# Retention's values two steps behind its scores, the convolution's norm beside the attention, and five smaller moves, in a three-block transformer kernel

## The chip, the cores and the metric

The kernel runs on one core of a Trainium2 chip. The metric is device time in microseconds (us) of one execution, median of three. Engine names: PE is TensorE (products), ACT is ScalarE (functions and copies out of PSUM), DVE is VectorE, POOL is GpSimd, SP issues most DMAs. PSUM has eight banks of 128x512 f32; a product writes a bank, and ACT or DVE empties it.

## What is computed

Sequence 512, width 1024. Two "hybrid" layers, then one block of another kind. A hybrid layer, cut to what matters here:

```python
def hybrid_layer(x, ...):
    u = rms_norm(x, g_mix_pre) @ w_in                 # aq ak av | cu | rq rk rv rg
    mix = concat([chunk_attention(aq, ak, av),        # 6 heads of 64
                  conv_module(cu), retention(rq, rk, rv, rg)]) @ w_out
    x = x + rms_norm(mix, g_mix_post)
    f = square(relu(rms_norm(x, g_mlp_pre) @ w_up)) @ w_down      # 4096 wide
    return x + rms_norm(f, g_mlp_post)

def conv_module(u):                                   # 256 channels, 31 taps
    y = causal_conv(a * sigmoid(gate)) + conv_b
    return silu(layer_norm(y) * ln_g + ln_b)

def retention(q, k, v, g):                            # 6 heads of 64, decayed causal scores
    q, k = rotary(q), rotary(k) / 8
    y = ((q @ k.T) * decay) @ v                       # what the chunked form amounts to
    return silu(g) * layer_norm(y)                    # one norm for each head
```

The last block has differential attention with 8 heads of value width 128 (each head's output is divided by its root mean square), a state-space layer whose parameters come from `exp`, `sin` and `cos` of small 128x16 tables and of their powers, gates, and an MLP.

## The kernel before

Each engine runs a program written out by hand (`products` for PE, `functions` for ACT, `arithmetic` for DVE, `low_parts` for POOL, `loads` for SP); semaphores join them. The order in which each function issues is the order on its engine, and an engine that waits holds back all that stands behind it on the same engine.

Large products are done in three passes of a reduced-precision form: weights and activations are both split in a high and a low part. SP loads a unit of weights (128x2048) to `raw`, ACT copies it to `w_hi` (`hi`, L1232), POOL subtracts to `w_lo` (`lo`, L509; for the very first unit in four pieces, `lo_pieces`, L501), and then PE may use it. There are two slots, so each chain load, copy, subtract of a unit runs beside the products of the unit before. For activations ACT writes `act_hi` and DVE `act_lo` (`split`, L1735; `low`, L1849).

**Start.** `first_norm` on ACT and the loop at the end of `arithmetic` on DVE take x in eight blocks k; `first_group` on PE (L762) does its first group k by k, twelve products for each k. At k = 7 it puts in the column means (L716) before output block 0 and the spread of the reciprocal root (`spread_rows`, L724) before output block 2. DVE's `turn_angles` (nine operations, L1920 to L1928) stands between block 1 and block 2. PE waits for `cmat`, a table of constant matrices, before its first product; its DMA is on ACT's queue behind block 1, and those of all eight x blocks are at ACT's start.

**Attention** of a hybrid layer is cut into steps i (head, query tile); `attention(i)` on each engine is put between pieces of the products for rq, rk, rv and rg (`attention_slots`), 26 slots and then the last steps together. Bank 3 is used by none of them while rq and rk are made.

**Retention** runs alone, with no large products beside it, until the first pieces of `w_out` (`OUT_STEPS`). Step i on PE: scores of step i into bank 4 or 5 (L771, `one`), values of step i - 1 (L798). Between them DVE multiplies the scores by `decay` out of PSUM into `pt` (L1807). The layer norms of the convolution (item 0) and of the three pairs of heads (items 1 to 3) are laid into the steps by `norm_steps`: mean on PE (L852), subtraction of the mean on DVE (L1860) and squares on ACT (L1389), variance on PE (L858), root on ACT and DVE, scaling, split. At step 2 DVE also splits the attention's three output blocks (L1849).

**MLP** of a hybrid layer: `up(g)` makes 512 hidden channels, `down(g)` adds their product with `w_down` to `f` in SBUF (L2023). In `up(0)` DVE clears `f` by a memset (L2013), and then runs `powers` (35 operations on 128x16, from L1939), the tables of the last block. It does so in both layers.

**Norms between parts** (`post_norm`): means, `busy(3)`, spread, `busy(12)`; `busy(n)` is n products of the identity with itself (L738) which nobody reads.

**Last block's attention**: for each step the scores, the turned probabilities (L1057, bank 6), the values (L1066), after a head's last step the mean of its squares (`one(6, m.avg128, ...)`, L771 with `att,cmat`, bank 6 too), and then `gate_piece(i)`, twelve large products.

```python
SEMAPHORE RULE, one(b, ...):  fill(b)            # wait until bank b was emptied
                              pe.matmul(...)     # then signal full<b>
retention, PE:   one(4 + i % 2, scores(i));  emptied(4 + (i - 1) % 2);  values(i - 1);  layer_norm(i)
```

## Time and profile before

| | us |
|---|---|
| median of 3 runs | 2418.72 |
| lowest, highest | 2415.46, 2423.01 |
| profiled execution, own time | 2415.07 |
| its span in the trace | 2413.2 |
| granted TensorE clock, mean | 0.965 of full |

Times below are in us from the span's start. A row of the timeline has start, duration, engine, line, operation, tiles and in brackets the idle time before it with what ended it. "x2" are two records; an f32 product shows as two. A product's duration is longer than its distance to the next, since products overlap; distances are what counts. 1.00 is PE's full clock (2.4 GHz), 0.50 its other level (1.2 GHz).

### The profile page before, as it was taken

To read this page: it belongs to the slowest core of one execution; us is meant where nothing else is said; L and a number is where in the kernel's file an instruction comes from. 1 tells how busy PE (TensorE), PEld (TensorE's weight loads), DVE (VectorE), ACT (ScalarE), POOL (GpSimd) and SP (SyncE) were. 2 spreads that over 40 slices of the span, in tenths; PEclk is the share of its full clock that TensorE was granted. 3 is DMA by queue.
4 is the path that set the end of the run, shared out by engine and by line. 5 is a ranking of instruction groups with operands and counts; after the bars stand their busy time and mean duration, and the time that the engine had idled before them with its cause. 6 is when DMAs were issued, how large, how long until landed. Compare 5 with 4: busy or idle time off the path is not lost.

```text
span 2413.2 us, 28705 instructions
## 1 busy us (share of the span) xinstructions
PE 2260.2 (94%) x10200; PEld 1729.8 (72%) x10200; DVE 1101.7 (46%) x1798; ACT 888.3 (37%) x1243; POOL 886.3 (37%) x274
## 2 busy tenths in 40 slices
PE   6999999999999998999999988977989789999999
PEld 4865487888878673778888866654766578788887
DVE  4844435221247444351222367674156652455445
ACT  4333343322343433532322332243255544333332
POOL 4522053343455221534444562321322135343443
PEclk9999899999999999999999998888999999999999
DMA  3412022323224220222232331011211113223232
GB/s 134 161 62 70 1 87 76 100 88 104 87 79 149 91 66 18 70 88 88 87 104 88 104 142 35 23 66 39 76 64 36 52 55 103 86 89 103 88 100 74
DMA packets 110587, 195.04 MB, mean 81 GB/s; under 512 B 4752, under 2 KB 41872, under 8 KB 110224
## 3 DMA queue, kind: packets, MB, share of 16 engines
q1 hardware_dynamic: 109184, 191.23, 24.2%
q10 hardware_dynamic: 1296, 2.43, 0.3%
q8 instruction: 63, 1.03, 0.2%
q14 instruction: 44, 0.36, 0.1%
HBM read 189.44 MB, written 8.12 MB: 82 GB/s over the span
## 4 chain that ended last, share of the span: by engine, by line
PE 69%; issue 21%; POOL 4%; DVE 4%; ACT 1%; DMA 1%; SPq 0%; POOLq 0%; DVEq 0%; ACTq 0%
PE bank L662 54%; POOL w_lo L509 4%; PE bank L771 4%; PE bank L762 3%; PE bank L798 1%; PE bank L835 1%; PE bank L959 1%; PE bank L826 1%; PE bank L858 1%; PE bank L716 1%; PE bank L738 1%; DVE b_pow L2076 0%; PE bank L990 0%; PE bank L852 0%; DMA lam<-in_lam 0%
## 5 line engine op out<-in xcount | busy, mean ns | idle before, releaser
L509 POOL TENSOR_TENSOR w_lo<-raw,w_hi 128x2048 fp32r<-128x2048 f32 (+1 forms) x167 | 740.4, 4434 | 1414.9 <-ACT w_hi L1232 1414.9
L662 PE MATMUL bank<-act_hi,w_hi 128*128 128x512 f32 x1488 | 605.9, 407 | 11.8 <-DVE act_lo L1849 4.4
L662 PE MATMUL bank<-act_lo,w_hi 128*128 128x512 f32 x1488 | 586.0, 394 | 0.0
L662 PE MATMUL bank<-act_hi,w_lo 128*128 128x512 f32 x1488 | 585.7, 394 | 0.0
L1232 ACT ACTIVATE w_hi<-raw 128x2048 fp32r<-128x2048 f32 (+1 forms) x170 | 314.1, 1848 | 641.5 <-PE bank L662 609.0
L662 PEld LDWEIGHTS bank<-act_hi,w_hi 128*128 128x128 f32 x1488 | 284.1, 191 | 93.8 <-issue 27.7
L662 PEld LDWEIGHTS bank<-act_lo,w_hi 128*128 128x128 f32 x1488 | 283.7, 191 | 63.6 <-issue 6.9
L662 PEld LDWEIGHTS bank<-act_hi,w_lo 128*128 128x128 f32 x1488 | 283.1, 190 | 61.1
L662 PE MATMUL bank<-h_hi,w_hi 128*128 128x512 f32 x736 | 298.7, 406 | 26.3 <-DVE h_lo L1849 17.7
L662 PE MATMUL bank<-h_lo,w_hi 128*128 128x512 f32 x736 | 294.6, 400 | 0.0
L662 PE MATMUL bank<-h_hi,w_lo 128*128 128x512 f32 x736 | 294.3, 400 | 0.0
L2023 DVE TENSOR_TENSOR f<-f,bank 128x512 f32<-128x512 f32 x128 | 87.4, 687 | 238.6 <-PE bank L662 238.6
L662 PEld LDWEIGHTS bank<-h_hi,w_hi 128*128 128x128 f32 x736 | 140.9, 191 | 66.3 <-DVE h_lo L1849 19.1
L662 PEld LDWEIGHTS bank<-h_lo,w_hi 128*128 128x128 f32 x736 | 141.1, 192 | 35.4 <-issue 1.5
L662 PEld LDWEIGHTS bank<-h_hi,w_lo 128*128 128x128 f32 x736 | 140.6, 191 | 35.0
L2008 DVE SCALAR_TENSOR_TENSOR hid<-bank,rrow 128x512 f32<-128x512 f32 x64 | 43.1, 690 | 233.8 <-PE bank L662 228.2
L762 PE MATMUL bank<-act_hi,w_hi 128*128 128x512 f32 x192 | 78.4, 408 | 27.1 <-POOL w_lo L501 16.8
L2300 DVE TENSOR_TENSOR bank<-bank,rrow 128x512 f32<-128x512 f32 x44 | 30.7, 699 | 142.7 <-PE bank L662 140.2
L525 POOL TENSOR_TENSOR sums<-sums,squares 128x512 f32<-128x512 f32 x50 | 64.9, 1298 | 46.4 <-ACT squares L1250 44.9
L1824 DVE CUSTOM_DVE_ANT_0 pr<-bank,btab 128x128 f32<-128x128 f32 (+3 forms) x48 | 23.6, 491 | 116.7 <-PE bank L771 116.0
L1784 DVE SCALAR_TENSOR_TENSOR bank<-ypad,lcol,bank 128x512 f32<-128x512 f32 x116 | 76.6, 750 | 0.0
L762 PE MATMUL bank<-act_hi,w_lo 128*128 128x512 f32 x192 | 76.5, 398 | 0.0
(321 smaller groups left out, 2835.8 us busy)
## 6 DMA issues: line engine op xcount, KB each, us to landing
raw<-in_w_up SPq DMA_DIRECT2D x32, 1024.0 KB, 5.1
raw<-in_w_down SPq DMA_DIRECT2D x32, 1024.0 KB, 5.1
raw<-in_w_in SPq DMA_DIRECT2D x26, 1024.0 KB, 5.2
raw<-in_w_up SPq DMA_DIRECT2D x44, 512.0 KB, 4.6
raw<-in_w_in SPq DMA_DIRECT2D x28, 768.0 KB, 4.5
raw<-in_w_out SPq DMA_DIRECT2D x12, 1024.0 KB, 5.1
raw<-in_w_down SPq DMA_DIRECT2D x22, 512.0 KB, 4.2
raw<-in_w_attn_proj SPq DMA_DIRECT2D x4, 1024.0 KB, 5.0
```

Source lines behind the costliest of these rows:

```text
L509: pool.tensor_tensor(m.w_lo[slot][:, 0:n], m.raw[slot][:, 0:n], m.w_hi[slot][:, 0:n].bitcast(F32), ALU.subtract).then_inc(s["split_ready"], 1)
L525: ins = pool.tensor_tensor(m.sums[:], m.sums[:], m.squares[n % 4][:], ALU.add)
L662: mm = pe.matmul(o, ll if i == 2 else lh, rl if i == 1 else rh, start=first and n == 0, stop=last and n == len(steps) - 1)
L716: mm = pe.matmul(bank[b][:, t:t + 1], x[:, t * P:(t + 1) * P], m.per_d, start=(part == 0), stop=(part == 1))
L738: pe.matmul(bank[1][:, 0:P], m.ident, m.ident, start=True, stop=True)
L762: mm = pe.matmul(bank[b][:], (wl if i == 2 else wh)[:, k % KU, cols], (m.act_lo if i == 1 else m.act_hi)[:, k, :], start=(k == 0 and i == ...
L771: pe.matmul(bank[b][:] if o is None else o, lhsT, rhs, start=True, stop=True).then_inc(s[f"full{b}"], 1)
L1232: act.activation(m.w_hi[slot][:, 0:n], m.raw[slot][:, 0:n], ACT.Copy).then_inc(s["w_hi"], 1)
L1784: ins = dve.scalar_tensor_tensor(to, y, w, sums, ALU.mult, ALU.add)
L2008: dve.scalar_tensor_tensor(m.hid[:, b, :], bank[b][:], 0.0, m.rrow[:], ALU.max, ALU.mult).then_inc(s[f"free{b}"], 1)
L2023: dve.tensor_tensor(sums, sums, bank[4 + b][:], ALU.add).then_inc(s[f"free{4 + b}"], 1)
L2300: dve.tensor_tensor(bank[b][:], bank[b][:], m.rrow[:], ALU.mult).then_inc(s["up_scaled"], 1)
```

## The change

- **Retention**: values stand two steps behind scores (`LAG = 2`), with scores in three banks in turn (4, 5, 1) and three buffers for the decayed scores (`pr`). The norms of the heads move by one step, the splits of items 1 and 2 by three more. The splits of the attention's output go to steps 5, 6 and 7, those of the convolution to 12 and 13.
- **Convolution's norm**: leaves retention's steps. Its mean, variance and root stand in attention steps 2, 4 and 6 with bank 3 (`conv_norm`); ACT's part with `Silu` (`conv_gate`) stands ahead of retention, in front of ACT's copy of the next weights.
- **Start**: x blocks 2 to 7 are loaded behind the directions and the first weight copy instead of at once, `tmul` on ACT's queue, `cmat` behind block 2. `turn_angles` stands before block 1, `powers` behind block 7, ahead of the reciprocal root. PE first does 14 products of `scol` which nobody reads, and waits for `cmat` only in `spread_rows`.
- **MLP**: `f` is cleared by two ACT copies with scale 0 behind `up(0)`'s last high part; DVE waits for them before its last low part. `powers` is gone from both layers.
- **Norms**: `busy(1)` in place of `busy(3)` between means and spread.
- **Last block**: the head's mean stands behind `gate_piece(i)` instead of before it.

```diff
 def retention():                                        # PE
-    one(4 + i % 2, m.rkT[...], m.rqT[...], bank[4 + i % 2][...])
-    if 1 <= i <= 6 * NT:
-        h, j = divmod(i - 1, NT)
+    one(SCORES[i % 3], m.rkT[...], m.rqT[...], bank[SCORES[i % 3]][...])
+    if LAG <= i < 6 * NT + LAG:
+        h, j = divmod(i - LAG, NT)
...
-        mm = pe.matmul(..., m.pt[:, (i - 1) % 2, 0:T - j * P], ...)
+        mm = pe.matmul(..., m.pr[:, (i - LAG) % 3, 0:T - j * P], ...)
...
+def conv_norm(i):                                       # PE; in attention steps
+    for stage in CONV_NORM.get(i, ()):
+        if stage in (MEAN, VARIANCE):
+            fill(CONV_BANK)
...
-NORM_BEGINS, NORM_STAGES = (1, 10, 18, 26), (0, 1, 3, 4, 7, 8)
+NORM_BEGINS, NORM_STAGES = (11, 19, 27), (0, 1, 3, 4, 7, 8)
+CONV_NORM = {2: (MEAN, CENTER), 4: (VARIANCE, ROOT), 6: (SCALE,)}
+Q_SPLIT, CONV_SPLIT = (5, 6, 7), (12, 13)
-BUSY = (3, 12)
+BUSY = (1, 12, 14)
...
+        if i < n_steps:                                 # PE, last block
+            gate_piece(i)
         if i >= 4 and (i - 4) % NT == NT - 1:
             pe.wait_ge(s["o_squared"], c.up("o_squared"))
             one(6, m.avg128, m.att[9][:])
-        if i < n_steps:
-            gate_piece(i)
...
+        conv_gate()                                     # ACT, ahead of retention
         hi()
...
+            if isinstance(g, int) and g == 0:           # ACT, up(0)
+                for half in range(2):
+                    act.activation(m.f[...4 blocks], m.eps.to_broadcast([P, 4 * T]), ACT.Copy, scale=0.0).then_inc(s["f_clear"], 1)
...
-            if isinstance(g, int) and g == 0:           # DVE, up(0)
-                link(dve.memset(m.f[:], 0.0))
-                powers()
...
     for k in range(KD):                                 # DVE, start
-        if k == 2:
+        if k == 1:
             turn_angles()
         split(k, new(k), gain("g0", m.scol, SC), False)
+    powers()
     root_row()
```

How it stands on the engines, at three places. First DVE's program at the start, before: `act_lo` is a split, `turn_102` to `turn_104` are work tiles of `turn_angles`.

```order
L1735 SCALAR_TENSOR_TENSOR act_lo<-bank,scol,act_hi 128x512 [waits act_hi,param_dve]
L1735 SCALAR_TENSOR_TENSOR act_lo<-bank,scol,act_hi 128x512 [waits act_hi]
L1920 TENSOR_TENSOR turn_102<-par,tmul 128x384
L1921 TENSOR_SCALAR turn_104<-turn_102 128x384 [waits param_dve]
L1922 SCALAR_TENSOR_TENSOR turn_102<-turn_104,turn_102 128x384 [waits param_dve]
```

The end of the same stretch after the change, still on DVE; L1984 is the last of `turn_angles`, L1995 the first of `powers`.

```order
L1984 SCALAR_TENSOR_TENSOR turn_table_68<-turn_104,turn_103 128x384 [waits param_dve]
L1777 SCALAR_TENSOR_TENSOR act_lo<-bank,scol,act_hi 128x512 [waits act_hi,param_dve]
L1777 SCALAR_TENSOR_TENSOR act_lo<-bank,scol,act_hi 128x512 [waits act_hi] x6
L1995 TENSOR_TENSOR par<-par 128x16 [waits param_act]
L1996 TENSOR_TENSOR par<-par 128x16 [waits dve_step]
```

So seven splits stand behind `turn_angles` where six did, and behind them, ahead of the reciprocal root, the 35 operations of `powers`.

Second, PE at retention's start, before (`pt,rv` are values, `rqT,rkT` scores, `conv,cmat` the mean of the convolution's norm):

```order
L771 MATMUL bank<-rqT,rkT 128x384 [waits free5]
L644 REGISTER_ALU
L649 REGISTER_ALU [waits free6]
L798 MATMUL bank<-pt,rv 64x512 [waits free4]
L852 MATMUL bank<-conv,cmat 128x512 [waits free2]
L852 MATMUL bank<-conv,cmat 128x512
L771 MATMUL bank<-rqT,rkT 128x256 [waits free4]
L649 REGISTER_ALU
L798 MATMUL bank<-pt,rv 64x384 [waits free5]
```

and after the change:

```order
L772 MATMUL bank<-rqT,rkT 128x512 [waits free4,rotated]
L644 REGISTER_ALU
L772 MATMUL bank<-rqT,rkT 128x384 [waits free5]
L772 MATMUL bank<-rqT,rkT 128x256 [waits free1]
L644 REGISTER_ALU
L799 MATMUL bank<-pr,rv 64x512 [waits free4,free6]
L772 MATMUL bank<-rqT,rkT 128x128 [waits free4]
L649 REGISTER_ALU
L799 MATMUL bank<-pr,rv 64x384 [waits free5]
```

Two scores now stand between a step's scores and its values, and the convolution's products are gone from here.

Third, PE at the end of the first head of the last block's attention, before: turned probabilities, values, the head's mean, the first of twelve products of the gate piece.

```order
L1057 MATMUL bank<-cmat,att_132 128x128 [waits free6,probs_scaled]
L1057 MATMUL bank<-cmat,att_132 128x128
L1066 MATMUL bank<-att_136,v_127 128x128 [waits probs_turned,free7]
L771 MATMUL bank<-att_139,cmat 128x512 [waits free6,o_squared]
L662 MATMUL bank<-act_hi,w_hi_54 128x512
```

After, from the last product of the gate piece on:

```order
L662 MATMUL bank<-act_hi,w_lo_56 128x512
L772 MATMUL bank<-att_139,cmat 128x512 [waits free6,o_squared]
L772 MATMUL bank<-k_97,q_96 128x128 [waits free4]
L772 MATMUL bank<-k_97,q_96 128x128 [waits free5]
L1066 MATMUL bank<-cmat,att_130 128x128 [waits free6,probs_scaled]
```

The twelve products moved from between the mean and the next step's turned probabilities, which share bank 6, to before the mean.

## Rows read from the trace of the kernel before

**Rows 1.** Page: busy time, share of span and instructions of each engine
```profile
PE 2260.2 (94%) x10200; PEld 1729.8 (72%) x10200; DVE 1101.7 (46%) x1798; ACT 888.3 (37%) x1243; POOL 886.3 (37%) x274
```

**Rows 2.** Waits of PE, whole span: us in total, times, longest
```profile
PE bank L771 <- ACTq L1617: 15.0, 7, 2.2
...
PE bank L662 <- POOL w_lo L509: 9.6, 3, 4.2
```

**Rows 3.** Timeline of PE, retention of layer 1: start, duration, operation, idle before
```profile
223.13 1.77 PE L771 MATMUL bank<-rqT,rkT 64*128 64x512 f32 x4
...
235.11 0.69 PE L798 MATMUL bank<-pt,rv 128*64 128x128 f32 x2 [3.63 <-DVE pt L1807]
...
265.71 1.12 PE L771 MATMUL bank<-rqT,rkT 64*128 64x512 f32 x2
...
270.39 1.12 PE L852 MATMUL bank<-rqT,cmat 128*128 128x512 f32 x2
...
272.44 1.12 PE L771 MATMUL bank<-rqT,rkT 64*128 64x512 f32 x2
...
280.15 1.13 PE L852 MATMUL bank<-rqT,cmat 128*128 128x512 f32 x2 [0.69 <-ACT rqT L1237]
```

**Rows 4.** Windows: stretch, length, busy of PE to POOL, granted clock, DMA
```profile
245.00:255.00 10.00, 10.00 (x16) 3.14 (x16) 4.79 (x8) 4.57 (x7) 0.00 (x0) 0.50 0.00 1
```

**Rows 5.** Timeline of DVE, retention of layer 1
```profile
228.68 0.43 DVE L1807 TENSOR_TENSOR pt<-bank,decay 128x256 f32<-128x256 f32 x1 [3.19 <-PE bank L771]
229.03 4.64 DVE L1849 TENSOR_TENSOR act_lo<-qT,act_hi 128x512 fp32r<-128x512 f32 x3
```

**Rows 6.** Timeline of POOL, retention of layer 1
```profile
227.41 4.50 POOL L509 TENSOR_TENSOR w_lo<-raw,w_hi 128x2048 fp32r<-128x2048 f32 x1 [2.59 <-ACT w_hi L1232]
```

**Rows 7.** Timeline of PE, retention of layer 2
```profile
906.09 1.77 PE L771 MATMUL bank<-rqT,rkT 64*128 64x512 f32 x4
...
956.87 1.12 PE L852 MATMUL bank<-rqT,cmat 128*128 128x512 f32 x2 [0.69 <-ACT rqT L1237]
```

**Rows 8.** Timeline of DVE, first `up` of layer 1's MLP
```profile
371.13 3.47 DVE L2013 MEMSET f<- 128x4096 f32 x1 [0.80 <-issue]
374.63 4.55 DVE L1939 TENSOR_TENSOR par<-par 128x16 f32<-128x16 f32 x1
...
386.63 2.48 DVE L2008 SCALAR_TENSOR_TENSOR hid<-bank,rrow 128x512 f32<-128x512 f32 x4 [0.24 <-issue]
```

**Rows 9.** Timeline of POOL, then of ACT, the same stretch
```profile
374.55 4.61 POOL L509 TENSOR_TENSOR w_lo<-raw,w_hi 128x2048 fp32r<-128x2048 f32 x1 [6.58 <-ACT w_hi L1232]
...
372.56 1.92 ACT L1232 ACTIVATE w_hi<-raw 128x2048 fp32r<-128x2048 f32 x1 [4.56 <-PE bank L662]
```

**Rows 10.** Timeline of PE, first `down` of layer 1's MLP
```profile
398.74 0.79 PE L662 MATMUL bank<-h_hi,w_hi 128*128 128x512 f32 x1 [4.14 <-POOL w_lo L509]
...
404.81 0.39 PE L662 MATMUL bank<-h_hi,w_lo 128*128 128x512 f32 x1
```

**Rows 11.** Timeline of ACT, then of DVE, start
```profile
12.19 1.91 ACT L1232 ACTIVATE w_hi<-raw 128x2048 fp32r<-128x2048 f32 x1 [2.85 <-DMA raw<-in_w_in]
...
15.93 1.16 DVE L1920 TENSOR_TENSOR turn<-par,tmul 128x384 f32<-128x384 f32 x1
...
30.65 0.56 DVE L1928 SCALAR_TENSOR_TENSOR turn_table<-turn,turn 128x384 f32<-128x384 f32 x1
```

**Rows 12.** Timeline of PE, start
```profile
32.05 0.79 PE L762 MATMUL bank<-act_hi,w_hi 128*128 128x512 f32 x1 [6.89 <-DVE act_lo L1735]
...
50.80 1.05 PE L724 MATMUL bank<-cmat,small 128*128 128x128 f32 x8
```

**Rows 13.** Timeline of PE, then of DVE, end of the last block's first head
```profile
1785.54 1.10 PE L771 MATMUL bank<-att,cmat 128*128 128x512 f32 x2 [2.15 <-ACTq L1617]
...
1789.73 0.55 PE L1057 MATMUL bank<-cmat,att 128*128 128x128 f32 x3
...
1788.72 0.75 DVE L1842 SCALAR_TENSOR_TENSOR att<-bank,kcol,att 128x512 f32<-128x512 f32 x1 [3.15 <-ACT att L1244]
```

200 lines of the change are left out of this document (118 added, 82 removed).

## The prediction

> **What bounds the kernel now.** I read the page first: PE is busy for 94% of the span, every other engine for under half [rows 1]. So the kernel goes at PE's pace, and an edit can pay in two ways only: by a wait of PE that goes, or by PE's clock. The second view is the list of PE's waits [rows 2], the third PE's timeline around each wait, read for the bracket (idle before, by whom) and for the distance from one product to the next, which doubles at half clock. The reader is to see that the change touches four places where PE waits or is slow: the start, retention, the first `down` of each MLP, and the head's mean in the last block. The sum is made against the profiled execution's own 2415.1.
>
> **Retention, the largest term.** In layer 1 it takes PE from 223.13 to 280.15, 57.0 us, in layer 2 from 906.09 to 956.87, 50.8 [rows 3, 7]. What would it take without waits and at full clock? One head of scores and values is 272.44 - 265.71 = 6.73 with a norm's mean of 1.12 in it, so 5.6; six heads 33.7. The two inner norms are four products of 1.12, 4.5; the convolution's norm four more of the same shape, 4.5; the wait ahead of the last mean is 0.7 [rows 3]. Together 43.4. So 13.6 are lost in layer 1 and 7.4 in layer 2, 21.0 in all. The loss has one beginning: PE waits 3.63 for the decayed scores of step 3 [rows 3], because DVE, in step 2, has three splits in its way which take 4.64 instead of some 2 [rows 5], and behind them the convolution's subtraction, which itself waits for PE. After the wait the granted clock is 0.50, the 1.2 GHz level, and ten microseconds later still, with PE never idle [rows 4]. The change takes both things away from the first steps: the splits go to steps 5, 6 and 7, one in each, the norm goes elsewhere, and a decayed score has two scores and a value more of PE's time (about 1.4 us a step, 5.6 over four) before it is wanted. What is late next? The copy of W_out's weights now stands behind `conv_gate` on ACT (two table loads, five `Silu`, two copies, about 7 us more), so POOL's 4.50 us subtraction moves from 227.4 [rows 6] into steps 8 to 11. No split stands there, and its user comes only at step 28. The bounds are the two waits alone without the clock, 7, and all of 21; I take 20, by the row at 265.71, where the same steps run tightly at full clock.
>
> What POOL does beside DVE matters in this change twice. The row shows that the 0.43 us decay product at 228.68, which reads PSUM, runs at its own speed while POOL subtracts, and the split at 229.03, with two inputs in SBUF, does not [rows 5, 6]. The Trainium skill (SBUF — State Buffer, section "SBUF: two separate sides") says why: DVE operations with two SBUF inputs and POOL's share a port pair under "an exclusive lock", held for a whole instruction. If the rule caught operations with one PSUM input too, each decay product that meets the moved subtraction would be held; the trace agrees with the rule as it stands.
>
> **The convolution's norm in the attention** costs PE its four products as before (they are in the 43.4 above, at full clock; they only change place). DVE gets 1.4 us in slot 2 and 2.9 in slot 6, ACT 1.2 and 2.0. DVE is busy for 46% and ACT for 37% of the span [rows 1], so there is room between steps, but an operation with two SBUF inputs can be held by a subtraction of 3.5, once or twice. I take +1 for both layers, from 0 to +5.
>
> **First `down` of each MLP.** DVE spends 3.47 on the memset and then 12.0 on `powers`, from 374.63 to 386.63, of which 4.55 is one operation held for POOL's 4.61 [rows 8, 9]. So `hid` of `up(1)` is late, ACT's copy behind it is late, POOL's subtraction too, and PE waits 4.14 at 398.74 and then runs 14 products in 6.07 us to 404.81 instead of 3.2 [rows 10]. Both edits take this away: 4.1 + 2.9 in layer 1. Layer 2 has the same wait (9.6 in three waits is 4.1 twice and 1.3 elsewhere [rows 2]) with a clock cost of 0 to 2.9; I take 1.4. What covers the moved memset? Two ACT copies of 128x2048, 1.92 each, 3.8, in ACT's 4.56 of idle time ahead of 372.56 [rows 9]: 0.7 to spare. Nothing else there is late then: `hid` can go as its banks fill. Sum 12.5, I take 12, from 8 to 13.
>
> **The start.** Two things are earlier and one is new. Weights: the first copy starts at 12.19 when its DMA has landed [rows 11]; with six x blocks (1.6 MB) behind it I estimate 8.5 to 9.5. Block 1's split now waits for `turn_angles`, nine operations, 15.3 us before (15.93 to 31.21), nearly all beside POOL, while the last, with POOL idle, took 0.56 [rows 11]. By my estimate they start at about 8.9 (block 0's split stands as it did), go fast until POOL starts at about 11.5, and then take 1.2 to 1.5 each: end at about 17.5, so PE is at block 1 at 18.3. From block 2 to the spread of the root it took 18.75 us (32.05 to 50.80 [rows 12]), 2.9 a block; so from block 1 21.6, and PE could spread at 39.9. The new thing is `powers`, 34 operations at 0.21 and one more [rows 8], behind block 7's split (about 27.5) and ahead of the reciprocal that the spread needs. Beside them POOL adds squares and then subtracts the third unit, 4.6 us, until about 34.5, and its lock lets through hardly one for each of its instructions, as at 374.63. They end at 41.4, and PE spreads at 41.6, 9.2 earlier than 50.80. It waits 2 to 4 us for it, for which I give back 1.7 of clock, as at 398.74. So -7.5. The bounds are -3 (turning tables held by POOL as before, and the clock) and -14 (`powers` hidden). DVE's taps and PE's products both hang on the same spread, so they shift together.
>
> **The smaller ones.** `busy`: two products fewer at four norms; four of the same width take 0.8 in the spread at 50.80 [rows 12], so at most 0.5 each, and the root may be what is waited for: -1, from 0 to -2. The 14 products at the start lie in PE's idle time: nothing, unless they raise the clock for block 0.
>
> **The head's mean.** PE waits 2.15 before it, seven times 15.0 [rows 2, 13], since bank 6 is not yet empty. With twelve products of 0.23 (2.8) before it the wait is covered, but the mean itself is some 0.5 later: it could begin at 1785.54 - 2.15 = 1783.4 and begins at 1783.4 + 2.8 = 1786.2. Bank 6 is needed again by the next step's turned probabilities, and is free only when ACT's three and DVE's first operation on the mean are done: 1788.72 + 0.75 = 1789.47, just ahead of 1789.73 [rows 13]. That chain hangs on the mean, so it ends at 1790.0, and what lay in between is now in front. The wait only changes place and grows: +0.3 to +0.6 each, seven times, +2.5, from 0 to +5.
>
> **Sum**: -20 + 1 - 12 - 7.5 - 1 + 2.5 = -37. 2415.1 - 37 = 2378. The profiled execution is at the low end of the runs (median 2418.7, lowest 2415.5), so for a median I add 1: 2379.
>
> **The rivals.** (1) Half a gain in retention: the clock falls there all the same, or a held split makes PE wait, in one layer. For it: in layer 1 the clock stayed low with PE busy all the time [rows 4], so a short wait is dear. Against: from 265.71 on nothing falls. It gives back 10: 2389. (2) `powers` hidden, because POOL's subtraction starts later or lets more through: the start gives 11 to 14 instead of 7.5, 2374. (3) The head's mean does what it seems to do, and 15 go: 2379 - 17.5 = 2361. Against it stands bank 6. (4) Slower. The clock is at its low level through both retention stages, from a first short wait on (POOL's moved subtraction on a split of steps 5 to 7 would do). Its 38.9 us of products then take twice that, 78, so 39 more a layer, 78 in all: 2457. It decides from half on: with 37 gained, slower begins where more than 37 of the 78 are lost. For it, rows 4, where work alone didn't raise the clock; against it, layer 2, where the same wait cost only 7.4 in all [rows 7], and the missing wait itself. (5) Retention and MLP do not pay, because another wait takes each one's place (a bank, ACT's copy behind `f_clear`): only the start is left, 2408 to 2415.
>
> **How the numbers follow.** My forecast, with the bounds of its terms, 0.60 (2368 to 2390); (1) 0.14; (2) 0.12; (3) 0.04; (4) 0.04; (5) 0.06. The range 2364 to 2395 takes in the forecast's bounds, (1) and (2), and leaves out (4), (5) and most of (3). A measurement tells 0.3%, 7 us, from no change. Faster by more is all but (4) and half of (5): 0.93; within it 0.03; slower 0.04.
>
> **What would show it.** In the changed kernel's trace: no idle bracket over 1 us on PE in retention, the granted clock 1.00 there, and about 39 us from its first score to the last mean; no wait at the first `down`; a wait of PE before the spread at about 41; the bracket of 2.15 gone from the head's mean, and one of about 3 before the next step's turned probabilities, by DVE's first operation on the mean. I am wrong if retention takes over 45 us, if the spread is before 38 or after 46, or if the last block's attention is shorter by more than 5.

## The result and the profile after

The changed kernel takes 2377.5 us (median of four runs, 2375.4 to 2382.6); the kernel before took 2417.1 beside it (2405.9 to 2423.0). The ratio is 0.9845, with a 95% interval of 0.9805 to 0.9884. The forecast was 2379, range 2364 to 2395. The profiled execution has a span of 2376.2 us against 2413.2, 37.0 less.

The page of the changed kernel, busy time of each engine and share of the span, which answers to [rows 1]:

```profile
PE 2248.2 (95%) x10212; PEld 1731.2 (73%) x10212; DVE 1078.8 (45%) x1761; ACT 895.4 (38%) x1247; POOL 886.2 (37%) x274
```

PE is still what bounds the kernel. It is busy 12.0 us less with twelve products more, and the rest of the 37.0, 25.0, is idle time that has gone. A total does not say where. I read one start time of PE at the border of each stage in both timelines, and took the differences. The stages are the same pieces of work in both kernels; only the convolution's norm has gone from retention to the attention.

| stretch of PE's timeline | before | after | gain |
| --- | --- | --- | --- |
| span's start to the attention's first score | 105.24 | 94.83 | 10.4 |
| layer 1, attention (with the products beside it) | 117.89 | 121.28 | -3.4 |
| layer 1, retention to its last mean | 57.02 | 38.32 | 18.7 |
| layer 1, column means to column means (norm, MLP) | 374.30 | 366.74 | 7.6 |
| from there to the attention's first score of layer 2 | 86.17 | 88.47 | -2.3 |
| layer 2, attention | 117.86 | 121.27 | -3.4 |
| layer 2, retention | 50.78 | 38.32 | 12.5 |
| layer 2, column means to column means | 371.57 | 366.71 | 4.9 |
| last block, from its first products to the attention's first score | 303.72 | 302.76 | 1.0 |
| last block's attention, to the last head's mean | 193.34 | 203.06 | -9.7 |
| last block, the rest, to PE's last product | 463.23 | 463.19 | 0.0 |

The stretches that are left out differ by about 0.1, and one more microsecond of the 37.0 lies behind PE's last product.

**Retention.** Windows of the changed kernel (stretch, length, busy of PE, PE's loads, DVE, ACT, POOL, then the granted clock, DMA share, GB/s). The first has the same times as the piece that ran at 0.50 before [rows 4], though the changed kernel is further on in its work by then; the others are retention of layer 1 and of layer 2:

```profile
245.00:255.00 10.00, 9.27 (x28) 3.42 (x27) 5.72 (x11) 3.69 (x6) 0.00 (x0) 1.00 0.01 2
216.11:254.43 38.32, 37.59 (x105) 13.16 (x104) 19.29 (x37) 18.32 (x26) 6.21 (x2) 1.00 0.09 28
878.54:916.86 38.32, 37.59 (x105) 13.16 (x104) 19.30 (x37) 18.32 (x26) 6.22 (x2) 1.00 0.08 28
```

The clock is full throughout, and PE is idle for 0.73 in 38.32. That is the one wait left, and it stood there before too [rows 3]:

```profile
254.43 1.12 PE L848 MATMUL bank<-rqT,cmat 128*128 128x512 f32 x2 [0.73 <-ACT rqT L1258]
```

DVE and POOL in layer 1's retention of the changed kernel, against [rows 5, 6] (start, duration, engine, line, operation, idle before):

```profile
223.49 0.68 DVE L1895 TENSOR_TENSOR act_lo<-qT,act_hi 128x512 fp32r<-128x512 f32 x1
...
224.43 0.68 DVE L1895 TENSOR_TENSOR act_lo<-qT,act_hi 128x512 fp32r<-128x512 f32 x1
...
225.63 0.68 DVE L1895 TENSOR_TENSOR act_lo<-qT,act_hi 128x512 fp32r<-128x512 f32 x1
227.23 4.51 POOL L509 TENSOR_TENSOR w_lo<-raw,w_hi 128x2048 fp32r<-128x2048 f32 x1 [9.42 <-ACT w_hi L1253]
227.27 0.69 DVE L1850 TENSOR_TENSOR pr<-bank,decay 128x512 f32<-128x512 f32 x1 [0.95 <-PE bank L772]
228.68 0.56 DVE L1850 TENSOR_TENSOR pr<-bank,decay 128x384 f32<-128x384 f32 x1 [0.72 <-PE bank L772]
```

The three splits take 0.68 each where they took 4.64 together (3.43, 0.68 and 0.68, so one of them was held), and are done before POOL begins. The decay products that meet POOL's 4.51 (227.23 to 231.74) take 0.69 and 0.56, exactly what the same shapes take without POOL (0.69 at 221.60, 0.56 at 223.02).

**First `down`.** The unit of weights that PE waited 4.14 for at 398.74 [rows 10] is subtracted by POOL in time, and PE takes it up without a wait and at full clock (PE, then POOL):

```profile
368.30 0.39 PE L662 MATMUL bank<-h_hi,w_hi 128*128 128x512 f32 x1
...
361.20 4.61 POOL L509 TENSOR_TENSOR w_lo<-raw,w_hi 128x2048 fp32r<-128x2048 f32 x1 [8.17 <-ACT w_hi L1253]
```

**Start.** PE, DVE and POOL in the changed kernel, against [rows 11, 12]:

```profile
17.89 0.80 PE L763 MATMUL bank<-act_hi,w_hi 128*128 128x512 f32 x1 [2.42 <-DVE act_lo L1777]
...
40.30 1.16 PE L725 MATMUL bank<-cmat,small 128*128 128x128 f32 x8 [1.19 <-DVE small L1763]
```

```profile
29.81 0.17 DVE L2003 TENSOR_TENSOR par<-par 128x16 f32<-128x16 f32 x1
30.02 4.50 DVE L1998 TENSOR_TENSOR par<-par 128x16 f32<-128x16 f32 x1
...
40.07 0.18 DVE L1763 RECIPROCAL small<-small 128x4 f32<-128x4 f32 x1
```

```profile
29.89 4.59 POOL L509 TENSOR_TENSOR w_lo<-raw,w_hi 128x2048 fp32r<-128x2048 f32 x1
```

Block 1 starts at 17.89 instead of 32.05, and the spread at 40.30 instead of 50.80. One operation of `powers` lies beside POOL's whole subtraction, and PE waits for DVE at the spread.

**The head's mean.** PE's waits in the changed kernel (engine, line, releaser: us in total, times, longest), against the 15.0 in seven waits of [rows 2], which are gone from the list. The first line is new; the second, the wait for the two sets of probabilities combined, was 11.7 in four waits before:

```profile
PE bank L1066 <- DVE att L1888: 18.3, 7, 3.0
...
PE bank L1066 <- DVE att L2294: 14.1, 6, 5.9
```

and the first of the seven in PE's timeline, with DVE's operation between, against [rows 13]:

```profile
1743.38 0.75 DVE L1888 SCALAR_TENSOR_TENSOR att<-bank,kcol,att 128x512 f32<-128x512 f32 x1 [3.51 <-ACT att L1265]
...
1744.28 0.52 PE L1066 MATMUL bank<-cmat,att 128*128 128x128 f32 x3 [2.56 <-DVE att L1888]
...
1746.94 0.77 PE L662 MATMUL bank<-act_hi,w_hi 128*128 128x512 f32 x1 [1.35 <-DVE gates L2275]
...
1752.01 0.70 PE L772 MATMUL bank<-k,q 64*128 64x256 f32 x4
```

The wait stands where the prediction put it. But behind it is a second wait, 1.35, and then the twelve products of the gate piece take 5.07 us (1746.94 to 1752.01), where twelve take 2.8 at full clock. A second wait at the gate piece stands behind three of the seven heads (1.35, 1.69 and 0.94).

### The profile page after: what moved, and what is told of

It is laid out like the page before. It is cut to its first block, busy times and chain, and to the rows that moved or that the text cites. A ratio compares the mean times of both kernels' runs of the same rounds, so it can differ in the third digit from the quotient of the medians.

```text
span 2376.2 us, 28595 instructions
## 1 busy us (share of the span) xinstructions
PE 2248.2 (95%) x10212; PEld 1731.2 (73%) x10212; DVE 1078.8 (45%) x1761; ACT 895.4 (38%) x1247; POOL 886.2 (37%) x274
## 4 chain that ended last, share of the span: by engine, by line
PE 72%; issue 19%; DVE 3%; POOL 3%; ACT 1%; DMA 1%; SPq 0%; ACTq 0%; POOLq 0%; DVEq 0%
PE bank L662 57%; PE bank L763 4%; PE bank L772 4%; POOL w_lo L509 3%; PE bank L836 1%; PE bank L799 1%; PE bank L968 1%; PE bank L827 1%; PE bank L716 1%; PE bank L725 1%; DVE b_pow L2128 0%; PE bank L999 0%; PE bank L998 0%; DMA lam<-in_lam 0%; PE bank L862 0%
## 5 line engine op out<-in xcount | busy, mean ns | idle before, releaser
L662 PEld LDWEIGHTS bank<-h_lo,w_hi 128*128 128x128 f32 x736 | 139.8, 190 | 35.3 <-issue 1.5
```

The costliest lines, as they stand in the source:

```text
L662: mm = pe.matmul(o, ll if i == 2 else lh, rl if i == 1 else rh, start=first and n == 0, stop=last and n == len(steps) - 1)
```

## The experiments

Each is the changed kernel with the edit shown. Since the stages repeat from kernel to kernel to a tenth of a microsecond where the clock is undisturbed, and single runs of the kernel before lie up to 0.8% apart, the verdicts rest on stretches of the timelines and not on totals, except where a ratio is given.

### The head's mean ahead of the gate piece again

```
-        if i < n_steps:
-            gate_piece(i)
         if i >= 4 and (i - 4) % NT == NT - 1:
             pe.wait_ge(s["o_squared"], c.up("o_squared"))
             one(6, m.avg128, m.att[9][:])
+        if i < n_steps:
+            gate_piece(i)
```

> The changed kernel with one edit undone: in the last block's attention the head's mean stands ahead of the gate piece again. From the first scores of that block's attention to its last product the kernel before took 193.3 us (1751.94 to 1945.28), the changed one 203.1 (1706.24 to 1909.30), so 9.7 more where I had put 2.5. My theory is that all of it comes from this order (the wait ahead of the turned probabilities, a second one ahead of the next gate piece, and the clock that falls after them): then this kernel takes 193 to 194 us there and the whole is 9 to 10 us shorter, some 2368. The rival: the 7 us above my term come from elsewhere (the stretch begins 46 us earlier against the DMA of the weights, or POOL's subtraction falls otherwise on DVE's operations); then only 2 to 3 us come back and the stretch takes about 200. PE waits ahead of the mean by 2.15 again, seven times.

Measured: 2366.9 (2363.2 to 2368.1), ratio to the kernel before 0.9815 (0.9781 to 0.9848). The stretch takes 193.29 us, as the 193.34 of before. Its waits and busy time, the windows of the kernel before, of the changed one, and of this one:

```profile
1751.94:1945.28 193.34, 161.37 (x767) 114.44 (x767) 119.06 (x300) 106.43 (x232) 36.60 (x8) 0.95 0.14 44
```

```profile
1706.24:1909.30 203.06, 165.95 (x767) 118.86 (x767) 121.92 (x300) 106.40 (x232) 36.55 (x8) 0.90 0.13 42
```

```profile
1706.08:1899.37 193.29, 161.30 (x767) 114.40 (x767) 119.03 (x300) 106.39 (x232) 36.57 (x8) 0.95 0.13 44
```

PE waits 2.15 ahead of the mean again, seven times. So the order alone makes the 9.7. With the same 767 products, 4.6 are busy time (165.95 - 161.37, at a clock of 0.90 instead of 0.95), and 5.1 are idle time (37.11 - 31.97). My term had counted the second kind only, and too little of it.

The size is that of most executions and not of all. Of the ten kernels with the changed order and the same code in this block, nine take 203.0 to 203.1 in the stretch, and one (two steps, splits in step 2, subtraction early, below) takes 199.2; the three with the old order take 193.2 to 193.3. So the order costs 5.8 to 9.9.

### The gate piece ahead of the turned probabilities

```
+            if early(i):
+                gate_piece(i)
...
-        if i < n_steps:
+        if i < n_steps and not early(i):
             gate_piece(i)
```

where `early(i)` is i >= 8 and i % 4 == 0, and with DVE's evacuation of the gate banks in the step before, ahead of `refine`.

> The changed kernel with the head's mean left behind the gate piece, but in the steps that follow a head's end the gate piece itself is put ahead of the turned probabilities, and DVE's evacuation of the four finished gate banks goes to the step before, ahead of the refinement. By the theory that in the changed kernel PE waits for the chain mean, ACT's three, DVE's first operation (2.56 to 2.98 ahead of the turned probabilities, then 1.35 ahead of the gate piece), the twelve gate products of 2.8 us now lie in that wait: about 2.5 us come off each of seven heads, with the clock's share of about 1 each more. The stretch of 203 us then takes 180 to 190, the whole kernel is 13 to 22 us shorter, 2355 to 2365, and shorter than with the mean ahead of the gate piece. The rival: bank 7 or the gate banks are then late instead (the gate products must find their bank emptied by DVE one step earlier, with POOL's subtraction holding DVE for 4.6), and the wait changes place again: 193 to 203 us, no better than the mean ahead of the piece.

Measured: 2372.1 (2367.5 to 2375.6), ratio 0.9839 (0.9803 to 0.9875). The stretch takes 196.3 us: better than the changed kernel by 6.8, worse than the plain old order by 3.0. The rival holds by its number. The 18.3 us of waits on the head's mean (L1888 there, L1894 here) are down to one of 3.0. The wait on L2294 is the one that the changed kernel had with 14.1, and two others are new in size:

```profile
PE bank L1072 <- DVE att L2294: 15.4, 8, 7.6
...
PE bank L1072 <- ACTq L1665: 7.2, 3, 2.9
...
PE bank L772 <- DVE small L2274: 3.3, 6, 0.6
```

But waits are not why this order is the worse one. Its window over the stretch, against the 193.29 above:

```profile
1707.03:1903.33 196.30, 165.03 (x766) 119.39 (x766) 115.72 (x300) 106.27 (x232) 36.47 (x8) 0.91 0.13 43
```

PE is idle for 31.27, no more than the 31.99 of the old order. It is busy for 165.03 against 161.30, at a granted clock of 0.91 against 0.95. So the rearrangement did take the new idle time away, and what it lost to the old order is clock.

### Retention: which part of the change took the wait away

Six kernels vary three things: the distance of the values (LAG), the step of DVE's three splits (`Q_SPLIT`), and whether ACT copies W_out's weights, and so POOL subtracts, ahead of or behind the convolution's gate.

Values one step behind:

```
-LAG, SCORES = 2, (4, 5, 1)
+LAG, SCORES = 1, (4, 5, 1)
```

> The changed kernel with the values of retention one step behind their scores instead of two; the three banks of scores, the moved splits and the moved norm stay. Read on the stretch from the attention's first score to retention's last mean, which took 174.9 us in layer 1 and 168.6 in layer 2 before, and 159.6 in both in the changed kernel. My account of the loss before was that three splits in one step and the convolution's norm behind them made PE wait 3.63 and the clock fall; the distance only gives slack. If the splits and the norm alone made the loss, this kernel takes 159 to 162 us in each. The rival: with one step's distance DVE's decay product (0.43 to 0.8 us, behind a split of 1.2) is late by some tenths in many steps, each with a wait of 0.2 to 1, and the clock falls in a part of them: 163 to 172.

All three as before, and only the norm moved:

```
-LAG, SCORES = 2, (4, 5, 1)
+LAG, SCORES = 1, (4, 5, 1)
-Q_SPLIT, CONV_SPLIT = (5, 6, 7), (12, 13)
+Q_SPLIT, CONV_SPLIT = (2, 2, 2), (12, 13)
-        conv_gate()
         hi()
+        conv_gate()
```

> The changed kernel with three parts of its retention as in the kernel before: values one step behind the scores, DVE's three splits all in step 2, and ACT's copy of the W_out weights ahead of the convolution's gate, so that POOL's subtraction stands at the start of retention. Only the convolution's norm stays in the attention. By my theory the wait comes from the three splits held beside POOL's subtraction (4.64 us for what takes some 2): PE waits 2 to 3.6 us at step 3 again, the clock falls behind it, and the stretch from the attention's first score to retention's last mean takes 165 to 171 us in layer 1 and 162 to 168 in layer 2 instead of 159.6. The rival: the norm in the first steps was what made the difference (its subtraction and PE's four products in steps 1 to 8 kept the clock down), and without it a single wait of some 3 us is all that is left: 162 to 163.

The weight copy ahead of the gate, alone:

```
-        conv_gate()
         hi()
+        conv_gate()
```

> The changed kernel with one order undone: ACT's copy of W_out's weights stands ahead of the convolution's gate again, so POOL's subtraction of 4.5 us falls into the first steps of retention; the three splits stay in steps 5 to 7, the values two steps behind. Retention, from its first score to its last mean, took 38.3 us in both layers of the changed kernel. In the kernel that had splits at step 2, values one behind and this order as before, one DVE group of three splits took 6.21 beside POOL's 4.82, PE waited 4.01 and then ran at 0.50 for 25 us in layer 1 and for the rest of retention in layer 2 (53.3 and 70.1). My theory: the splits have to meet the subtraction for that. From 222.8 to 227.3 POOL would be at work in steps 2 to 5, so only the first split (step 5) can meet its end; the two steps of slack (some 2.8 us) hide it: 38 to 39 in both. The rival: any of DVE's operations beside POOL is held, PE waits 1 to 3 us and the clock falls: 45 to 70.

The splits in step 2, alone:

```
-Q_SPLIT, CONV_SPLIT = (5, 6, 7), (12, 13)
+Q_SPLIT, CONV_SPLIT = (2, 2, 2), (12, 13)
```

> The changed kernel with DVE's three splits all in step 2 of retention again, but POOL's subtraction still late (behind the convolution's gate) and the values two steps behind. By my theory the three splits without POOL beside them take about 2 to 2.5 us (three of 0.6 to 0.7, each behind ACT's copy), and with two steps of slack PE hardly waits: retention 38 to 40 us in both layers, against 38.3. The rival: three splits in one step are too many by themselves (they wait for ACT's three copies, 1.67 us, which run while the first scores do), PE waits 1.5 us or more at the value of step 2 or 3, and the clock falls to its lower level as before: 45 or more in one of the layers.

The last two edits together:

> The changed kernel with both of the two things that did nothing alone undone together: DVE's three splits all in step 2 of retention, and ACT's copy of W_out's weights ahead of the convolution's gate, so that POOL's subtraction meets them. Values stay two steps behind their scores, the norm stays in the attention. With values one step behind this pair gave a wait of 4.01 and 53.3 and 70.1 us of retention. By my theory the meeting of splits and subtraction makes the wait, and the second step is slack of a value and a score, some 1.5 us: PE waits 2.3 to 2.8 at the value of step 3, and since the clock fell after waits of 2.7 and more at the start, it may fall here too: 41 us if it stays, 50 to 70 if it falls; I expect the fall. The rival: two steps of distance alone were enough to hide the splits (the change's own description names them first); then 38.3 to 39 in both layers.

One step, splits in step 2, subtraction late (and another edit at the start, below):

> The changed kernel with values one step behind and DVE's three splits all in step 2 of retention, but the copy of W_out's weights (and with it POOL's subtraction) still behind the convolution's gate; and, in another stretch, with DVE's nine operations of the turning angles ahead of block 2 instead of block 1 at the start. In retention, by my theory, splits without POOL beside them take 2 to 2.5 us instead of 6.21, PE waits under 1 at the value of step 3, and the two retentions take 39.6 to 41 us (39.6 was measured with one step and the splits apart). The rival: three splits in a step are too long for one step's distance by themselves, and the clock falls: 45 or more. At the start PE waited 2.42 ahead of block 1 for DVE; with the angles one block later that wait should shrink to under 1 or move to block 2, and the first scores of the attention come 0 to 2 us earlier than 96 to 98, where the other kernels with powers at the start had them; the rival there is that the end of DVE's row of work is what counts, and nothing changes.

What was measured, us from the first score to the last mean, and the whole kernel's time (one run each, but for the changed kernel):

| values behind by | splits in step | POOL's subtraction | layer 1 | layer 2 | whole |
| --- | --- | --- | --- | --- | --- |
| 2 | 5, 6, 7 | late (the changed kernel) | 38.32 | 38.32 | 2377.5 |
| 2 | 5, 6, 7 | early | 38.32 | 38.33 | 2376.3 |
| 2 | 2 | late | 38.33 | 38.33 | 2378.0 |
| 2 | 2 | early | 38.32 | 38.32 | 2380.9 |
| 1 | 5, 6, 7 | late | 39.59 | 39.58 | 2380.3 |
| 1 | 2 | late | 39.58 | 39.57 | 2383.4 |
| 1 | 2 | early | 53.30 | 70.12 | 2426.1 |

(One step with the splits apart and the subtraction early was not run.) Two steps instead of one are worth 1.3 us a layer by themselves. The loss is there only in the last line. In that kernel, PE, DVE and POOL in layer 2:

```profile
899.05 0.43 DVE L1850 TENSOR_TENSOR pr<-bank,decay 128x256 f32<-128x256 f32 x1 [1.34 <-PE bank L772]
899.40 6.21 DVE L1894 TENSOR_TENSOR act_lo<-qT,act_hi 128x512 fp32r<-128x512 f32 x3
...
899.63 4.82 POOL L509 TENSOR_TENSOR w_lo<-raw,w_hi 128x2048 fp32r<-128x2048 f32 x1 [2.58 <-ACT w_hi L1253]
...
905.86 0.69 PE L799 MATMUL bank<-pr,rv 128*64 128x128 f32 x2 [4.01 <-DVE pr L1850]
```

and its windows, all of retention, and ten microseconds of it 40 us behind the wait:

```profile
895.35:965.47 70.12, 65.19 (x105) 19.82 (x105) 24.08 (x38) 18.32 (x26) 6.52 (x2) 0.57 0.04 15
945.00:955.00 10.00, 10.00 (x16) 3.36 (x16) 4.45 (x8) 0.63 (x1) 0.00 (x0) 0.50 0.00 0
```

One wait of 4.01, and PE, not idle again until 0.7 ahead of the last mean, stays at 1.2 GHz to the end of the stage. DVE's three splits take 0.68, 5.01 and 0.68: one of them is held. That is the fourth rival of the prediction, at 32 us for this layer: it had the place and the mechanism, and it costs more than the whole gain of the change's retention. The same 4.01 in layer 1 cost 15. (1.3 of each is the one step's own.) So the move of the norm by itself gives nothing: attention and retention together take 174.6 in layer 1, against 174.9 before, and 191.4 in layer 2, against 168.6. The one run of this kernel took 2426.1, more than the kernel before. The convolution's norm is not needed for the loss either, since the wait and the low clock are there without it.

The kernel with both of the harmless edits undone (two steps, splits in step 2, subtraction early) was expected to lose, and does not. Its DVE and POOL rows say why:

```profile
220.89 1.89 DVE L1894 TENSOR_TENSOR act_lo<-qT,act_hi 128x512 fp32r<-128x512 f32 x3
222.56 4.61 POOL L509 TENSOR_TENSOR w_lo<-raw,w_hi 128x2048 fp32r<-128x2048 f32 x1 [2.58 <-ACT w_hi L1253]
```

With two steps, the scores of step 2 come a value earlier, and the third split is under way when POOL begins; the group takes 1.89, as it does without POOL (1.88 in the kernel with a late subtraction). The second step doesn't hide the collision here: the third split begins at 222.09, 0.47 ahead of POOL, so there is none. It is a matter of half a microsecond. The kernel with the splits apart and the subtraction early shows what slack can do: there one split is held for 1.98 instead of 0.68, and PE does not wait.

```profile
226.72 1.98 DVE L1895 TENSOR_TENSOR act_lo<-qT,act_hi 128x512 fp32r<-128x512 f32 x1
```

### The convolution's norm back in retention

```
-CONV_NORM = {2: (MEAN, CENTER), 4: (VARIANCE, ROOT), 6: (SCALE,)}
+CONV_NORM = {1: (MEAN,), 2: (CENTER,), 4: (VARIANCE,), 5: (ROOT,), 8: (SCALE,)}
```

with `conv_norm(i)` in retention's steps, the gate behind step 8, and so ACT's copy of W_out's weights, and POOL's subtraction, early.

> The changed kernel with the convolution's norm back in retention (its mean, subtraction, variance, root and scaling in steps 1, 2, 4, 5 and 8, its gate behind that), W_out's weight copy ahead of it; values two steps behind and splits in steps 5 to 7 stay. The four products of the norm cost the attention 3.4 us there (117.9 before, 121.3 in the changed kernel). By my theory their place is worth nothing by itself: retention takes 38.3 + 3.4 = 41.7 to 43 us and the attention 117.9, so both together 159.6 to 161 as in the changed kernel (159.6). The rival: the norm's subtractions and ACT's squares and root in the first steps are what made DVE late before, beside POOL's subtraction, so that PE waits a microsecond or more and the clock falls: both together 163 or more.

Measured: 2408.0 in its one run; attention 117.86 and 117.84, retention 53.97 and 53.16, both together 171.8 and 171.0 against 159.6. It is the rival by its number, and by mechanism neither the rival nor my theory. PE has no wait over 0.3 in the steps where the norm's products are; it waits at step 11, ahead of the first inner norm:

```profile
241.48 2.08 PE L849 MATMUL bank<-rqT,cmat 128*128 128x512 f32 x2 [4.72 <-ACT rqT L1258]
```

and ACT, from 235 on:

```profile
235.41 1.52 ACT L1439 ACTIVATE conv<-conv,lcol 128x512 f32<-128x512 f32 x2 [5.21 <-DVE conv L1934]
236.84 1.13 ACT L1357 ACTIVATE act_hi<-conv 128x512 fp32r<-128x512 f32 x2
237.88 1.65 ACT L1445 ACTIVATE gT<-gT 128x512 f32<-128x512 f32 x3
239.53 1.28 ACT L1446 ACT_TABLE_LOAD   x1
240.83 0.60 ACT L1258 ACTIVATE rqT<-bank 128x512 f32<-128x512 f32 x1
```

ACT waits for the norm's scaling, does the whole gate, and only then copies the first pair of heads, for which PE waits. With values two steps behind, that pair is ready one step later than in the kernel before, where the copy stood ahead of the gate. So two steps of distance and a norm in retention don't go together in this arrangement; whether another place of the gate would make them, and the norm's place then be worth nothing, stays open.

### The MLP's first `up`: memset or powers

Powers back in the MLP, the memset on ACT:

```
             if isinstance(g, int) and g == 0:
+                powers()
...
-    powers()
```

> The changed kernel with DVE's 34 operations of powers back in the first up of both MLPs, and the memset still on ACT. Before, DVE had 3.47 of memset and 12.0 of powers there, and PE waited 4.14 at the first down, so some 11.4 us of such work would be free. By that count powers alone leave a wait of 0.6 and next to nothing of clock: from the mean columns behind retention to those at the layer's end 367 to 368.5 us, against 366.7 in the changed kernel and 374.3 and 371.6 before. The rival: powers are what is late (POOL's lock holds their first operation by 4.5), and the wait and the low clock are there again: 371 or more. At the start the spread of the root comes without them some 2 us earlier, at 38 to 39 instead of 40.3, if it is DVE that it waits for there.

The memset back on DVE, powers at the start:

```
-            if isinstance(g, int) and g == 0:
-                for half in range(2):
-                    act.activation(m.f[...], ..., scale=0.0)
...
+            if isinstance(g, int) and g == 0:
+                dve.memset(m.f[:], 0.0)
```

> The changed kernel with the memset of the MLP's sum back on DVE (3.47 us), and powers still at the start. By the same count (11.4 us of DVE work are free ahead of the first down) the memset alone costs nothing: no wait at the first down, and 366.7 to 367.2 us from the mean columns behind retention to those at the layer's end, in both layers. The rival: the memset is long and stands right ahead of the banks that up(1) wants emptied, so PE waits 1 us or more: 368 to 371.

Measured, from column means to column means: with powers 369.88 and 368.88, with the memset 365.86 and 365.82 (2377.1 in all, one run), in the changed kernel 366.74 and 366.71. So with the powers gone the memset's move is worth nothing, as expected. With the memset gone the powers are worth 2.2 to 3.1, more than the count allowed (a wait of 0.6), since PE waits 1.88 and 1.90:

```profile
368.28 0.49 PE L662 MATMUL bank<-h_hi,w_hi 128*128 128x512 f32 x1 [1.88 <-POOL w_lo L509]
```

The two do not add up to what both cost together: the kernel before, which had both there, took 7.6 and 4.9 more than the changed one, with a wait of 4.14 and 4.16. So while the powers are there, the memset ahead of them is worth the rest, 4.4 and 2.7. Moving the powers away is enough by itself; moving the memset away takes a good half.

The powers' price is at the start. There the kernel with powers in the MLP has no wait before the spread, which stands at 38.86, and the attention's first score comes at 93.30. In the nine other kernels with an unchanged start it comes at 96.5 to 98.9. (The changed kernel's own profile, 94.83, is the best of all of these, and the one in which PE's first blocks ran as here.) So moving `powers` gained 5.3 in the two MLPs, and cost 1.5 at the start by the nearest pair of executions and up to 5.6 by the others. In all the kernel takes 2378.3 in its one run, no more than the changed one; part of that are the stretches with the norms behind the MLPs, which vary from execution to execution and were 1.7 and 2.2 shorter in it.

### The start: powers behind the root, and the turning angles one block later

Powers behind the root, with the head's mean ahead of the gate piece as in the first experiment, as a candidate for the best version:

```
-    powers()
     root_row()
     ...
+    powers()
```

> A candidate for the best version: the changed kernel with the head's mean ahead of the gate piece again (that gave 193.3 instead of 203.1 us in the last block's attention), and with the operations of powers at the start moved behind the root row of the first norm, so that the spread of the root doesn't wait for them. Without powers at the start at all, the attention's first score came at 93.3, against 94.8 to 98.8 in the kernels that had them ahead of the root. I expect 93.3 to 94.5 here too, no wait at the MLPs' first down (366 us from mean columns to mean columns), and 2360 to 2364 in all, 13 to 17 less than the changed kernel. The rival: powers then stand ahead of the convolution's tables and the taps, and POOL's lock holds one of them for 4.6; the attention's first steps wait for what is behind, and the start is no better than 96 to 98: 2367.

Measured: 2374.8 (2372.0 to 2377.0), ratio 0.9852 (0.9829 to 0.9875). The last block's attention takes 193.23, so the first experiment holds a second time. The start is worse than in all the kernels above: the spread comes at 38.96 without a wait, but the attention's first score at 100.81.

```profile
52.62 0.80 PE L662 MATMUL bank<-act_hi,w_hi 128*128 128x512 f32 x1 [5.76 <-DVE ypad L2022]
```

The rival holds, with a wait larger than it had: `powers` behind the root makes DVE late for `ypad`, the convolution's input, which it writes out of PE's banks. In this arrangement DVE has less slack between the root and the taps than ahead of the root.

The turning angles ahead of block 2, in the kernel with one step and a late subtraction (expectation above):

```
-        if k == 1:
+        if k == 2:
             turn_angles()
```

Here the wait didn't shrink, it grew and moved to block 2:

```profile
27.82 0.80 PE L763 MATMUL bank<-act_hi,w_hi 128*128 128x512 f32 x1 [8.17 <-DVE act_lo L1777]
```

The spread comes at 47.23 and the attention's first score at 101.68, 2.8 to 5.2 later than in the nine kernels with the changed start. One operation of the nine was held for POOL's whole instruction, and it has one input in SBUF only:

```profile
19.92 4.53 DVE L1980 TENSOR_SCALAR turn<-turn 128x384 f32<-128x384 f32 x1
```

The same operation on the same shape took 0.36 at 26.02, with POOL idle. In the changed kernel the nine begin at 8.50, and four of them are through and the fifth has begun before POOL's first addition at 10.85. With the angles one block later 3.6 of the start's 6.3 to 8.7 are left, so about half of the gain is the place of the angles.

## Why the prediction was right, and where it was not

The total was met, 2377.5 against 2379. That it was met so closely is luck: retention gave 5.3 more than its term and the start 2.9 more in the profiled execution, and the head's mean cost 7.2 more. Against the sum's terms:

- **Retention and the norm**, forecast -19 (-20 and +1), measured -24.3 (-15.3 in layer 1, -9.0 in layer 2). The mechanism was right, that is, splits beside POOL's subtraction, one wait, then the clock; the clock is full in both layers. The term was mis-sized in its floor. I took 43.4 for the same products without waits; it is 38.3 + 3.4 = 41.7, since the four products of the norm take 3.4 beside the attention and not 4.5, and a head 5.5 and not 5.6. That is 1.7 a layer, 3.4 (the 5.5 is the mean over the six, 38.3 less the wait of 0.7 and four products of 1.12; in the middle of the stage a head takes 5.66). I also took 1 less than the floor gave, and gave 1 to the norm's work on DVE, which cost nothing. The argument on slack (a decayed score has two scores and a value more) was right in that no wait came, but the runs showed that it wasn't what decided: the second step alone, or the late subtraction alone, was enough, each by keeping splits and subtraction apart. Whether spreading the splits alone is enough was not run; with two steps it let one held split through without a wait.
- **The rule on POOL's lock.** The decay products that read PSUM ran at their own speed beside the moved subtraction (0.69 and 0.56), so it did no harm there. The Trainium skill (SBUF — State Buffer, section "SBUF: two separate sides") names, beside DVE operations with two SBUF inputs, those in a two-port performance mode as taking the lock. The trace agrees: a TENSOR_SCALAR with one SBUF input took 4.53 instead of 0.36 at the start of the kernel with the later angles. (0.36 is less than the 0.56 of two-input operations on that shape, so such a mode is likely; the trace has no field that names it.) I had weighed only the first kind.
- **First `down` of each MLP**, forecast -12, measured -12.4 (-7.6 and -4.9). Right, and both edits belong to it as I had said, but they do not add: the powers' move alone takes all of it; the memset's alone, by the kernel before against the one with only the powers back, 4.4 and 2.7.
- **The start**, forecast -7.5, measured -10.4 in the profiled execution; the kernels with the same start lie at -6.3 to -8.7. The place of block 1 (18.3 forecast, 17.89 found), of the spread (41.6 and 40.30, with 40.3 to 41.6 in the others) and the one operation of `powers` under POOL's whole subtraction were as said. What differs is the wait at the spread: 1.19 in the profile, with the clock staying full, and 2.7 to 4.0 in the others, with the clock at its lower level behind it. The spread is set by DVE, and PE came to it later in the profile, with block 7 begun at 37.50 against 35.3 to 36.8, because its clock had fallen behind the wait of 2.42 at block 1. So the extra gain here is a matter of the execution, and the others lie on both sides of the forecast.
- **The head's mean**, forecast +2.5, measured +9.7. This is the step that failed. "The wait only changes place and grows: +0.3 to +0.6 each" followed one chain (mean, ACT, DVE, turned probabilities), and that chain does end where I put it. It left out the work queued on DVE behind `refine`: the head's output, the masked scores, and the four gate banks' evacuation, for which PE waits again. And it left out the clock. At the old place, the wait of 2.15 left the clock alone four times in seven (the products of the mean take 1.10 then, and 1.54 to 1.85 in the other three); at the new place it fell within 2 us behind five of the seven, and where 2.56 and 1.35 end 2.7 us apart, the products behind them run at half speed. I knew the clock's price from the MLP and used it there. Of the 9.7, 5.1 are waits and 4.6 are clock.
- **The smaller ones**: nothing in the profile can be put down to `busy`. The stretch behind layer 1's MLP, where two of the four norms are, is 2.3 longer in the changed kernel, and takes between 85.5 and 91.4 in the kernels that share its code there, against 86.17 before. It goes with the clock there: 85.5 to 86.9 at a mean of 0.98, 88.0 to 89.8 at 0.96, 91.4 at 0.94.

The signs by which I said I would be wrong did not come (retention over 45, the spread before 38 or after 46), except that the last block's attention moved by more than I had a limit for, on the side where I had set none.

The best version that was run is the changed kernel with the head's mean left where it was: 2366.9, and 9.8 us less than the changed kernel in the one stretch that differs.

## What to carry to other kernels

Price a wait of the bounding engine with what its clock does afterwards, and ask what other wait will stand close to it; a wait that "only changes place" is not free. When several edits are made against one stall, the stall may be a collision of two instructions on two engines, and an edit that parts them can be enough, even by half a microsecond: look for the pair before building slack. A move that relieves one stage is paid where the work lands, so read the slack of the new place, as with `powers`, which gave 5.3 in the MLPs and cost 1.5 to 5.6 at the start. And when two edits relieve one wait, undo each alone: here the whole was 12.4, and the two taken back one at a time gave 5.3 and 0.

## What the runs showed of the hardware that I had not expected

The price of the same wait varied widely from one place of the trace to another. After 4.01 before the same product, PE ran at half clock for 24 us in layer 1 and for 65 in layer 2 (the clock missing in windows of 5 us, summed and doubled), in one execution and with the same instructions behind it. In the kernel before it was 24 us in layer 1 and 7 in layer 2, after 3.63 in both, and in the kernel with the norm in retention 17 and 14, after 4.72. In the longest case PE, idle for only 0.7 in the 60 us, did not get its clock back in all of retention, and got it back among the large products that follow. The granted clock was 0.50 in the window of 945 to 955 shown above, and this is the window of the 14.5 us behind retention:

```profile
965.47:980.00 14.53, 14.53 (x50) 10.85 (x51) 6.06 (x9) 3.22 (x5) 0.00 (x0) 0.84 0.01 1
```

Ahead of the spread at the start a wait of 1.19 left the clock full and waits of 2.7 to 4.0 brought it down. What decides how long it stays down is not settled by these runs.
